# A forget-gate attention in two passes, and dot products that read one operand from PSUM

## What is computed

```python
q, k, v, g, f = jnp.split(h @ w_in, [FOX_W, 2 * FOX_W, 3 * FOX_W, 4 * FOX_W], axis=-1)
q = _rms_norm(q.astype(jnp.float32).reshape(b, s, FOX_HEADS, FOX_HD), q_gain).transpose(0, 2, 1, 3) * (FOX_HD ** -0.5)
...
log_f = jax.nn.log_sigmoid(f.astype(jnp.float32) + b_f.astype(jnp.float32))
cum = jnp.cumsum(log_f, axis=1).transpose(0, 2, 1)
...
    logits = (jnp.einsum('bhqd,bhkd->bhqk', q[:, :, qs:qe], k[:, :, :qe])
              + cum[:, :, qs:qe, None] - cum[:, :, None, :qe])
...
    p = jax.nn.softmax(jnp.where(causal, logits, -jnp.inf), axis=-1)
    outs.append(jnp.einsum('bhqk,bhkd->bhqd', p, v[:, :, :qe]))
...
return (o.astype(h.dtype) * jax.nn.silu(g)) @ w_out
```

## Time and profile before

| | us |
|---|---|
| median of three runs | 3806.01 |
| the profiled execution | 3800.73 |
| its span, first to last instruction | 3798.9 |
| TensorE (PE) busy | 3085.4 |
| its weight loads (PEld) busy | 1984.0 |
| VectorE (DVE) busy | 1835.6 |
| GpSimd (POOL) busy | 1189.4 |
| ScalarE (ACT) busy | 935.9 |

### The profile page before, as it was taken

How to read it: one execution, slowest core, us unless ns; L and a number is a source line. 1 busy time by engine, 2 the same in 40 slices (tenths; PEclk the granted TensorE clock), 3 DMA queues, 4 the chain that set the end, 5 groups by cost and what they waited for, 6 DMA issues and landing times. The chain is left out here.

```text
span 3798.9 us, 32596 instructions
## 1 busy us (share of the span) xinstructions
PE 3085.4 (81%) x10941; PEld 1984.0 (52%) x10941; DVE 1835.6 (48%) x3465; ACT 935.9 (25%) x1750; POOL 1189.4 (31%) x1224
## 2 busy tenths in 40 slices
PE   6999898987776968957779998867777787787878
PEld 3787564853345836837678876723333333333333
DVE  2532523224333233633335244577867856875444
ACT  1112212153322284351212323211111111111111
POOL 0000000002210000002331000077777777777775
PEclk8999998995678988988989999978888888898888
DMA  5332141310012200200001223199999999999998
GB/s 190 100 100 77 56 175 53 100 45 2 0 34 89 89 0 24 96 20 1 0 0 45 89 89 139 53 385 405 402 405 419 413 411 419 410 410 419 419 419 346
DMA packets 227043, 697.69 MB, mean 184 GB/s; under 512 B 22002, under 2 KB 24290, under 8 KB 226530
## 3 DMA queue, kind: packets, MB, share of 16 engines
q0 software_dynamic: 147456, 536.94, 35.1%
q1 hardware_dynamic: 79476, 159.43, 12.3%
HBM read 690.00 MB, written 6.29 MB: 183 GB/s over the span
## 5 line engine op out<-in xcount | busy, mean ns | idle before, releaser
L2043 DVE CUSTOM_DVE_ANT_0 proj_banks<-u_rows,h 128x1024 f32<-128x1024 f32 x512 | 630.4, 1236 | 420.6 <-DMA u_rows<-in_peer_u_dram,eidx 420.2
L2024 POOL DMA_INDIRECT u_rows<-in_peer_u_dram,eidx x512 | 496.7, 970 | 592.6 <-DVEq L2065 436.7
L2119 PE MATMUL work_banks<-v_rows,diag 128*128 128x512 f32 x1024 | 506.2, 658 | 184.8 <-ACT diag L2110 184.8
L218 DVE TENSOR_TENSOR weights_low<-weights_raw,weights_high 128x2048 fp32r<-128x2048 f32 x108 | 247.6, 2292 | 568.9 <-ACT weights_high L213 557.9
L2119 PEld LDWEIGHTS work_banks<-v_rows,diag 128*128 128x128 f32 x1024 | 214.6, 213 | 475.3 <-issue 405.1
L2119 PE MATMUL work_banks<-x_res,diag 128*128 128x512 f32 x512 | 285.5, 721 | 140.5 <-ACT diag L2110 139.0
L1044 POOL TENSOR_SCALAR fox_lg<-fox_lg,fox_sm 128x128 f32<-128x128 f32 (+1 forms) x64 | 68.3, 1084 | 1035.7 <-DVE fox_sm L1024 1035.7
L213 ACT CAST weights_high<-weights_raw 128x2048 fp32r<-128x2048 f32 x108 | 206.2, 1909 | 696.0 <-PE proj_banks L276 643.4
L276 PE MATMUL proj_banks<-h_low,weights_high 128*128 128x512 f32 x896 | 352.8, 394 | 26.2 <-PEq L589 13.6
L276 PE MATMUL proj_banks<-h_high,weights_high 128*128 128x512 f32 x896 | 352.3, 393 | 0.0
L276 PE MATMUL proj_banks<-h_high,weights_low 128*128 128x512 f32 x896 | 352.2, 393 | 0.0
(11 more groups left out here) (371 smaller groups left out, 4719.8 us busy)
## 6 DMA issues: line engine op xcount, KB each, us to landing
weights_raw<-in_w_in_dram SPq DMA_DIRECT2D x36, 1024.0 KB, 5.1
mod_w<-in_mod_w_dram SPq DMA_DIRECT2D x24, 1024.0 KB, 13.3
weights_raw<-in_ret_w_in_dram SPq DMA_DIRECT2D x24, 1024.0 KB, 5.3
weights_raw<-in_fox_w_in_dram SPq DMA_DIRECT2D x16, 1024.0 KB, 5.4
weights_raw<-in_ret_w_out_dram SPq DMA_DIRECT2D x8, 1024.0 KB, 5.1
weights_raw<-in_peer_w_q_dram SPq DMA_DIRECT2D x8, 1024.0 KB, 5.1
u_rows<-in_peer_u_dram,eidx POOLq DMA_INDIRECT x512, 7.6
x_res<-in_x_dram SPq DMA_DIRECT2D x2, 2048.0 KB, 12.1
```

The lines of the kernel that those rows point to most:

```text
L218: nc.vector.tensor_tensor(wlo[h][:, :, :], raw[h][:, :, :], whi[h][:, :, :].bitcast(F32), ALU.subtract).then_inc(w_split[h], 1)
L2024: nc.gpsimd.indirect_dma_start(out=ur[:, s, e, :] if table is u_tab else v_row(s, e), out_offset=None, in_=table, in_offset=bass.IndirectO ...
L2043: nc.vector.tensor_tensor_reduce(out=trash[:, e % 2, :], in0=ur[:, g % 2, e, :], in1=h3[:, t, :], scale=1.0, scalar=0.0, op0=ALU.mult, op1 ...
L2119: last = nc.tensor.matmul(pa[:, 2 * (t % 2) + half, :], diag[:, s, e, :], v_row(s, e)[:, half * CW:(half + 1) * CW], start=(first and e == 0),
```

## The change

Three things change.

1. *Projections of the forget-gate layer.* The forget columns are loaded twice, into columns 0 to 15 and 32 to 47 of a cleared block of 48, split into high and low and multiplied by `passes`: 24 matmuls. The running sum is kept as high and low part in one tile (`ncum_r`) and transposed (`ncum_t`). The gate is projected with tokens on the partitions. The head norm moves inside the projections: its steps stand between half chunks of chunks 4 to 6. So does a first pass of the attention: between the half chunks 6.1, 7.0 and 7.1 TensorE makes all logits (product of q and k, diagonal mask by a product with the identity, running sum by a product with a selector), and VectorE takes only the negated maxima. These are transposed and split (`nmax_r`).
2. *Attention, second pass.* The logits are made again, transposed: keys on the partitions, the maxima added by the selector. ScalarE's exponential reads PSUM, adds the running sum as a bias and writes the weights as the values product wants them. Ten products of 128 x 65 per head give output and sum (v carries a column of ones). VectorE divides and gates (`gate`). Two heads' output is transposed (`turn`), split by ScalarE and VectorE, and is the input of `output`, which no longer splits. GpSimd has no part in it. Scores and transposes take turns in six PSUM banks.
3. *Experts.* The token rows of a tile are copied to PSUM banks 2 and 3 of `pa` (`place_rows`), and the dots read them there. The weighted sums of all tiles use banks 0 and 1, so each tile waits for `add_rows` of the one before, which now stands behind the first group.

```diff
+                        def logits(h):
+                            rows = slice((h % 2) * FOX_HD, (h % 2 + 1) * FOX_HD)
+                            m = h // 2
+                            pe.wait_ge(scaled, 2 * m + 2)
+                            for t in range(TT):
+                                i, width = TT * h + t, (t + 1) * P
+                                if i >= 4:
+                                    pe.wait_ge(max_ready, i - 3)
+                                else:
+                                    pe.wait_ge(ln_done, 2 * PAIRS)
+                                nc.tensor.matmul(pa[:, t, 0:width], qk[rows, m, t * P:width],
+                                                 qk[rows, PAIRS + m, 0:width], start=True, stop=False)
+                                nc.tensor.matmul(pa[:, t, t * P:width], ident_r[:, :], diag_r[:, :],
+                                                 start=False, stop=False)
+                                nc.tensor.matmul(pa[:, t, 0:width], sel[:, h, :], ncum_r[:, 0:width],
+                                                 start=False, stop=True).then_inc(lg_full, 1)
+
+                        pe.wait_ge(wf_ready, 1)
                         for k in range(KT):
+                            last = passes(pa[0:ROWS, 0, :], wf_r[:, 0, k, :], wf_r[:, 1, k, :], parts[0][:, k, :],
+                                          parts[1][:, k, :], True, k == 0, k == KT - 1)
                         last.then_inc(f_full, 1)
...
+                        project_half(pe, 4, 0, parts, False)
+                        project_half(pe, 4, 1, parts, False)
+                        head_squares(0)
+                        project_half(pe, 5, 0, parts, False)
+                        head_squares(1)
+                        project_half(pe, 5, 1, parts, False)
+                        head_squares(2)
+                        project_half(pe, 6, 0, parts, False)
+                        head_squares(3)
+                        project_half(pe, 6, 1, parts, False)
+                        for h in range(0, 8):
+                            logits(h)
+                        project_half(pe, 7, 0, parts, False)
+                        for h in range(8, H):
+                            logits(h)
+                        project_half(pe, 7, 1, parts, False, range(0, 2))
+                        pe.wait_ge(max_spread, 1)
+                        for t in range(TT):
+                            last = nc.tensor.transpose(pa[0:ROWS, 0, t * P:(t + 1) * P], nmax[:, t, :], ident)
+                        last.then_inc(nm_full, 1)
+                        project_half(pe, 7, 1, parts, False, range(2, 4))
...
+                        def maxima(h):
+                            for t in range(TT):
+                                dve.wait_ge(lg_full, TT * h + t + 1)
+                                nc.vector.tensor_reduce(nmax[:, t, h:h + 1], pa[:, t, 0:(t + 1) * P], AX, ALU.max,
+                                                        negate=True).then_inc(max_ready, 1)
...
+                        for c in range(1, n):
+                            split_second(high, c)
+                            if c == 4:
+                                act.wait_ge(ncum_ready, 1)
+                                squares(0)
+                            elif c == 5:
+                                roots(0)
+                                squares(1)
+                            elif c == 6:
+                                roots(2)
+                                squares(3)
+                            split_next(high, c)
+                            if c == 5:
+                                roots(1)
+                                squares(2)
+                            elif c == 6:
+                                roots(3)
...
+                                if j < 3:
+                                    bank_free("scores", h, j)
+                                out_tile = scores_of(h, j)
+                                nc.tensor.matmul(out_tile, qk[rows, PAIRS + h // 2, j * P:(j + 1) * P],
+                                                 qk[rows, h // 2, j * P:S], start=True, stop=False)
+                                nc.tensor.matmul(out_tile[:, 0:P], diag_r[:, :], ident_r[:, :],
+                                                 start=False, stop=False)
+                                nc.tensor.matmul(out_tile, sel[:, h, :], nmax_r[:, j * P:S],
+                                                 start=False, stop=True).then_inc(st_full, 1)
+
+                        def values(h):
+                            if h >= 2:
+                                pe.wait_ge(o_read, h - 1)
+                            for t in range(TT):
+                                if t == 0:
+                                    pe.wait_ge(exp_done, TT * h + TT)
+                                for j in range(t + 1):
+                                    last = nc.tensor.matmul(pa[:, 2 + h % 2, t * VW:(t + 1) * VW],
+                                                            weights(h, j, t, t + 1), v[:, j, h, :],
+                                                            start=(j == 0), stop=(j == t))
                             last.then_inc(o_full, 1)
...
+                        def turn(pair):
+                            bank_free("pair", pair)
+                            pe.wait_ge(o_read, 2 * pair + 2)
+                            for t in range(TT):
+                                last = nc.tensor.transpose(bank_of("pair", pair)[:, t * P:(t + 1) * P],
+                                                           sg[:, t, pair * P:(pair + 1) * P], ident)
+                            last.then_inc(tr_full, 1)
+
+                        scores(0)
+                        for h in range(H):
+                            if h + 1 < H:
+                                scores(h + 1)
                             values(h)
+                            if h % 2 == 0 and h >= 2:
+                                turn(h // 2 - 1)
+                        turn(PAIRS - 1)
+
+                    @block.scalar
+                    def _(act):
+                        def exps(h):
+                            if h >= 2:
+                                act.wait_ge(o_full, h - 1)
+                            for j in range(TT):
+                                act.wait_ge(st_full, TT * h + (j + 1 if j < 2 else TT))
+                                nc.scalar.activation(weights(h, j, j, TT), scores_of(h, j), ACT.Exp,
+                                                     bias=ncum_t[:, j, h:h + 1]).then_inc(exp_done, 1)
...
+                        def gate(h):
+                            o = pa[:, 2 + h % 2, 0:TT * VW].rearrange("p (t d) -> p t d", t=TT)
+                            dve.wait_ge(o_full, h + 1)
+                            nc.vector.reciprocal(rinv[:, h, :], o[:, :, FOX_HD]).then_inc(rinv_ready, 1)
+                            dve.wait_ge(rinv_ready, h + 1)
                             for t in range(TT):
+                                cols = slice(h * FOX_HD, (h + 1) * FOX_HD)
+                                last = nc.vector.scalar_tensor_tensor(sg[:, t, cols], o[:, t, 0:FOX_HD],
+                                                                      rinv[:, h, t:t + 1], sg[:, t, cols],
+                                                                      ALU.mult, ALU.mult)
+                            last.then_inc(o_read, 1)
+
+                        def low_of(pair):
+                            dve.wait_ge(tr_high, pair + 1)
+                            nc.vector.tensor_tensor(out_parts[1][:, pair, :], bank_of("pair", pair),
+                                                    out_parts[0][:, pair, :].bitcast(F32), ALU.subtract
+                                                    ).then_inc(tr_low, 1)
+
+                        for h in range(H):
...
                             nc.vector.tensor_tensor_reduce(
-                                out=trash[:, e % 2, :], in0=ur[:, g % 2, e, :], in1=h3[:, t, :],
+                                out=trash[:, e % 2, :], in0=ur[:, g % 2, e, :], in1=hp,
                                 scale=1.0, scalar=0.0, op0=ALU.mult, op1=ALU.add,
                                 accum_out=dots[:, g % 2, e:e + 1]).then_inc(dot_done, 1)
+
+                    def place_rows(t):
+
+                        dve.wait_ge(dot_done, PRE + t * NG * GE)
+                        for half in range(2):
+                            cols = slice(half * CW, (half + 1) * CW)
+                            nc.vector.tensor_copy(hp[:, cols], h3[:, t, cols]).then_inc(h_placed, 1)
+                        dve.wait_ge(h_placed, 2 * t + 2)
...
                     for t in range(TT):
+                        place_rows(t)
                         for g in range(NG):
                             scores_of(t, g)
+                            if t and g == 0:
+                                add_rows(t - 1)
...
```

(12 more changed lines are left out.)

369 lines of the change are left out of this document (209 added, 160 removed).

## The result

Four runs of the changed kernel took 3846.1 to 3849.4 us, median 3848.7; the kernel before, run beside them, 3801.3 (median). The ratio is 1.0127, with a 95% interval of 1.0111 to 1.0143: slower by 1.3%, where 3650 was forecast. One of the four runs of the kernel before took 3961.25 us, in a slower state of the chip, and is left out of the ratio. The profiled execution took 3848.3 us, its span 3846.5.

A forecast was written before the change was run, and what follows sets the result against it. The prediction took the attention to be bound by its handover chain at a low clock and the expert stage by GpSimd's issue. Sum: 3800.7 − 122.8 − 29 = 3648.9, said as 3650 us; range 3612 to 3712.

The forecast's parts named there:

- ring of handovers: Old forget-gate attention: logits, maximum, exponential, scaling, transpose, copy, values in a chain, 15.8 us per head, no engine full.
- (a): Forget product: 3.6 us of delay, then 24 split products in 7.1 us instead of 15.5; projections start at 633.6.
- (b): Projections of the forget-gate layer: 768 products as before, 176.5 us.
- (c): Head norm inside the projections: 43.4 us go, 13.8 us of TensorE products of ones come.
- (d): First pass of logits: 3.4 us per head, 54.4 us for 16, plus one stall of 1 us.
- (f): Second attention pass: 6.3 us per head, 100.8 for 16 and 5 behind; output starts at 990.5, 122.8 us earlier.
- the clock stays low: Rival for the second pass: clock granted 0.60 as in the old attention, 70 us more, 3720 us; chance 0.09.
- The two stretches cited against it: Small products with TensorE 91% busy at clock 1.00, and the kernel's other attention, 82% busy at 0.92.
- The mark on which this was to be judged: Sign in the second pass: over 9 us per head would prove the forecast wrong.
- (g): Expert-stage dots reading PSUM: gathers take 1282 us instead of 1313, about 2 more at the tail; 29 us saved.
- PSUM frees nothing: Rival for the expert stage: something else holds the gathers, or DMA engines take over the bound; 3679 us, chance 0.10.

The follow-up runs named there:

- filler: Changed kernel with the selector product issued four more times ahead of every 64-row logit product, same result: 3927.1 us on a chip where the kernel before takes 3949.
- pad: Changed kernel with 128-row logit products against GpSimd's copies of each head's keys, other 64 rows zero, same result: 3652.3 us, ratio 0.9628 to the kernel before.
- rows128: Changed kernel with the logit products of both passes over all 128 rows instead of a head's 64, each holding two heads' summed logits: 3650.7 us.

## Why the prediction was wrong, step by step

*What bounds the kernel:* right on what the change removes. The ring of handovers went (5 us of waits on TensorE in the whole layer instead of 63 in the attention), and dots that read PSUM hold no gather up. The rule of the Trainium skill that spoke against this (SBUF — State Buffer, Who interferes with whom: a two-input VectorE instruction takes only the read side and descriptor generation needs the write side, which it calls inferred) isn't borne out here: 31.4 us of delay in dots with both inputs in SBUF, none with one in PSUM. The same section of the Trainium skill also says that a VectorE instruction with two inputs in SBUF contends with a GpSimd instruction that reads SBUF. A gather takes its row numbers (`eidx`) from there, so the rows agree with this rule; which side of the pair it was they don't show.

*(a)* 7.3 us for the forget product, forecast 7.1; its delay of 3.6 us did not come, and the projections start at 629.4 instead of 633.6. *(b), (c)* From there to the first logits are 170.7 us; the forecast's terms up to that place (14 half chunks of 11.04, 13.8 of sums of squares, 1.6 of small transposes) make 170.0. No wait stands ahead of L938. Right.

*(d)* **The first failed step: "3.4 us per head, 54.4 us".** The two halves of the first pass take 65.7 us (800.1 to 865.85) and 65.4 (878.25 to 943.64), 131.1 in all, 8.2 to 8.6 a head: 76 us more than forecast with its stall. The price of the eight logit products, 2.25 us, was read from a group that took 2.42. In that attention nine of the sixteen groups took 4.63, at the low clock, the very next head's among them, and I took the price at full clock for a stage in which TensorE would not wait:

```profile
1009.05 4.63 PE L971 MATMUL proj_banks<-fox_qk 64*128 64x128 f32 x8
```

Beside this the change between 64 and 128 rows, 1.1 us a head at full clock, had no price. What the runs showed in place of 3.4 us: 8.56 at 0.50 with 64 rows, 4.37 at 1.00 with 64 rows (filler), 3.24 at 1.00 with 128 (pad).

*(f)* **The second, and larger: "the second pass 6.3 us per head with a clock above 0.9".** It ran from 957.85 to 1170.93, 213.1 us instead of 106, at 0.50. The reasoning was that the low clock of the earlier trace rows came from idle time and would go with it. The idle time went and the clock fell further, from 0.60 to 0.50; with products of 128 rows it was 1.00. The rival "the clock stays low" named the outcome, but for the wrong cause (short idles between banks) and at a third of the price: it left out the first pass and kept a fifth of the second at full clock. The two stretches cited against it, 1825 to 1850 and 1375 to 1475, were no fair witnesses: their products span 128 rows. The mark on which this was to be judged, over 9 us per head, was passed at 13.

The Trainium skill (TensorE: Matmul & The Clock Gate, What's actually happening) says that the gate follows how busy TensorE has been, default low and released by activity. The rows agree only if busy means more than having a product under way: with TensorE busy 185 us of 185 the granted clock was 0.50, and giving the same instructions 128 rows instead of 64 made it 1.00.

With that one cause removed the steps stand. In pad a head takes 3.24 us where (d) had 3.4, and 5.66 where (f) had 6.3, output starts at 974 where the forecast had 990, and the kernel takes 3652 us where it had 3650. That last closeness is luck: the forget-gate layer came out 16 us better, what lies between it and the first gather 3.5 worse and the expert stage 15 worse.

*(g)* **Mis-sized: "about 2 us more at the tail; I take 29".** The gathers take 1279.6 us, forecast 1282; the tail grew by 20.2 us, and the stage gained 13.5. The rate was right: 419 GB/s from 2560 to 3815. Two things were missing in the sum. At each of the three changes of tile a result goes out and token rows come in, 0.52 MB each: by estimate 7.5 us at 419, and in the view of DMA issues the time to landing rises by some 3 us at each. And the end is uneven, 26 GB/s for over 11 us. A backlog of under 2 us was forecast and one of 22 came. The rival "PSUM frees nothing, because the DMA engines take over the bound" was half true.

By sum: 3648.9 + 180.4 (output at 1170.9 instead of 990.5) + 3.5 (from there to the first gather, 1353.1 us instead of 1349.7) + 15.5 (expert stage) = 3848.3, the profiled time.

## What to carry to other kernels

Before a low granted clock is put down to idle time, look at the shapes of the products in that stretch: here, with products of 64 rows among them, TensorE stayed at 1.2 GHz while it was busy for every microsecond, and filling the rows with zeros, or even adding useless 128-row products, made the kernel faster. A price read from a timeline has two levels where the clock alternates; say which level the new stage will be granted and from what row, and let a witness have the same shape. And when an issuer that feeds the DMA engines near their rate is made faster, count every byte that moves in the stage, and look at whether the time to landing grows and at what rate the last bytes come.

## What the runs showed that was not expected

- Rows that hold only zeros bring the same clock as rows that hold data (pad and rows128 both at 1.00, 3652 and 3651 us).
- Four idle products of 128 rows ahead of each logit product, 2.9 us of work per head and pass, saved 72 us; one each saved 30.
- Going from 128 to 64 rows and back costs some 0.28 us at full clock (4.37 instead of 3.24 us for a head with four such pairs of changes). That the change, and not something else in the mixture, is the cause was argued from the timelines and not tried by itself.
- On one chip GpSimd waits over 150 us between its gathers; it takes 3949 us for the kernel before, where the others took 3793 to 3806. What it waits for stayed open.
- At the end of the expert stage a sixteenth of the DMA rate (26 of 419 GB/s) goes on for over 11 us alone, once GpSimd issues without delay.
